# The output and router stage and the expert stage of a decoder layer as one program

## Chip, cores and metric

One Trainium2 chip, one of its cores. The metric is the device time of one execution, in microseconds.

## What is computed

One step of a one-layer decoder for 512 prompt tokens and 8 x 8 sample tokens, 576 in all, with 1,024 features, in float32. Two token mixers work side by side, their outputs are concatenated and projected, and a mixture of experts follows. What matters here, cut from the reference:

```python
y = jnp.concatenate([gla_o, nsa_o], axis=-1) @ w_out          # output projection
xp = xp + mod_p[:, 2] * yp
hp2 = modulate(xp, g_ffn[l], mod_p[:, 3], mod_p[:, 4])        # norm, scale, shift
logits = h @ w_router + b_router                              # 32 experts
top_logit, top_idx = lax.top_k(logits, 4)
top_w = softmax(top_logit)
# the token/expert pairs are sorted by expert into blocks of 128 rows; for each block:
gate = jnp.minimum(xb @ w_gate[e] + b_gate[e], 7)
up = jnp.clip(xb @ w_up[e] + b_up[e], -7, 7)
y = ((up + 1) * gate * sigmoid(1.702 * gate)) @ w_down[e] + b_down[e]
# rows are weighed and added up per token, then the residual and a last norm
```

Each expert has three matrices of 1,024 x 1,024. An expert with more than 128 rows needs a further, "overflow", block.

## The kernel before

`STAGES` (L3281) lists seven stages. Each issues its instructions inside a block of its own and ends with `stage_done` (L123 to 127), which clears its semaphores and makes all engines wait for each other. The change concerns the last two.

**`output_and_router` (L2212).** Tokens come in five tiles (`TILES`): four of 128 rows and a last one of the 64 sample rows. TensorE goes through the tiles: `project_out(t)` (L2387) makes the second half of the output columns (L2398; for the last tile both halves, in two column groups, L2401), then for the tile before it `turn_rows` (L2404, eight transposes), `route` (L2409, the logits, with the turned rows as stationary operand, L2416) and for the one before that `ranks` (L2420, how many earlier rows chose the same expert). VectorE adds the residual (L2657 to 2660), multiplies by the scale (L2665), chooses the tile before's experts (`choose`, L2587), finishes the norm (L2671), then does `shares`, `take_rank` and `place` (L2602 to 2636): the latter writes 0/1 matrices that say which expert and which row of a block each token goes to. ScalarE copies the turned rows (L2509) and makes the norm's root and the softmax's exponents. Products of the 0/1 matrices (`table`, L2457 to 2464) give the table of tokens by block; `begin_sums` (L2445) makes the sum over a token's experts of share times `b_down`, which starts each row of the result in DRAM. After the table VectorE counts the blocks (L2695 to 2710): from the number of rows per expert it works out which expert each overflow block belongs to and how many blocks are used. GpSimd gathers block 0's rows from DRAM (L2369), and SyncE asks for the first six quarters of the expert weights (L2342) once all projections are done and the last tile is normed.

**`experts` (L2750).** One step per block. The weights stream from DRAM in quarters of 1 MB, twelve per block, into six landing places. Each quarter is rounded by ScalarE (`high_part`, L3079), the remainder is taken by VectorE (`rest_part`, L3167), and TensorE makes three products from it: 12 instructions of 512 columns per quarter (L2965). The two halves of a split quarter stand in a ring of four, so rounding quarter n waits until quarter n-4 is used. Step k on TensorE is: biases, the four gate quarters, the turns of the activation of block k-1 (L2973), the four up quarters, the turns of the rows of block k+1, the four down quarters of block k-1. VectorE also reads the gate (L3180) and the up product (L3186), makes the activation (L3191, L3194) and the remainders of the turned rows (L3171). Before step 1 there is an opening in which block 0's gate and up products are made, and `overflow` (L3015) makes the table entries of the overflow blocks, from matrices that `place_overflow` (L2191) writes. The loop's length and the experts of the overflow blocks are read from SBUF (`used_blocks`, L2829). With this input 32 blocks are used.

## Time and profile before

| | us |
|---|---|
| median of three runs | 1798.55 |
| lowest, highest | 1796.72, 1801.39 |
| the profiled execution, own time | 1795.53 |
| its span, first to last instruction | 1793.5 |
| mean granted TensorE clock | 0.964 |

The page of the profile gives each engine's busy time; the chain of waits gives what ended last; the windows give busy time, granted clock (1.00 is 2.4 GHz, 0.50 is 1.2 GHz) and DMA for a stretch; the timeline gives the instructions in order, with like ones merged. All times are from the start of the span.

### The profile page before, as it was taken

What the parts mean: (1) busy time and instruction counts of PE and PEld (TensorE: products, weight loads), DVE (VectorE), ACT (ScalarE), POOL (GpSimd) and SP (SyncE); (2) the same over time, 40 slices, a digit from 0 to 9 for tenths busy, and PEclk for the clock granted to TensorE, in tenths of its full rate; (3) what the DMA queues carried; (4) which work ended last, traced back from release to release, by engine and by line L of the source; (5) the groups of instructions that cost most, each with busy time, mean ns of one, the idle gap of its engine ahead of it and who ended that gap; (6) DMA issues with size and microseconds to landing.
All of it is one profiled execution on the core that took longest, in us unless ns stands there. A gap on an engine that the chain in (4) does not pass through costs nothing.

```text
span 1793.5 us, 27031 instructions
## 1 busy us (share of the span) xinstructions
PE 1688.0 (94%) x9028; PEld 1312.8 (73%) x9028; DVE 1425.5 (79%) x1361; ACT 1099.8 (61%) x1045; POOL 333.4 (19%) x309
## 2 busy tenths in 40 slices
PE   4999978888998799999999999999999999999996
PEld 2776767555554478888888888888888888888884
DVE  4422564476426789999999999999999999999997
ACT  4212343455333367777777777777777777777773
POOL 0000021300101012223222222322222232223211
PEclk9999989699999689999999999999999999999998
DMA  9454553620226579999999999999999999999993
GB/s 348 172 185 171 107 156 101 209 96 7 77 87 200 219 269 355 382 371 377 375 378 376 371 377 376 373 375 375 378 371 381 377 373 376 382 374 374 386 351 125
DMA packets 114598, 516.08 MB, mean 288 GB/s; under 512 B 25870, under 2 KB 47710, under 8 KB 62058
## 3 DMA queue, kind: packets, MB, share of 16 engines
q1 hardware_dynamic: 101082, 483.48, 71.5%
q0 software_dynamic: 12800, 29.45, 5.9%
q10 hardware_dynamic: 656, 2.36, 0.3%
q8 instruction: 36, 0.59, 0.1%
q14 instruction: 24, 0.20, 0.0%
HBM read 502.75 MB, written 31.09 MB: 298 GB/s over the span
## 4 chain that ended last, share of the span: by engine, by line
PE 62%; DVE 1%; DMA 1%; ACT 0%; issue 0%; SPq 0%; POOL 0%; DVEq 0%; POOLq 0%; ACTq 0%
PE banks L2965 58%; PE banks L2973 3%; PE banks L2951 1%; DMA routing<-in_g_final 0%; DMA ffn_rows<-weighed,block_rows 0%; DVE split L3167 0%; DVE arena L3264 0%; PE banks L3020 0%; ACT split L3079 0%; DVE arena L3257 0%; DVE arena L3256 0%; SPq L2885 0%; POOL wait_taken L2903 0%; DVEq L2831 0%; DVE gates L3180 0%
## 5 line engine op out<-in xcount | busy, mean ns | idle before, releaser
L2965 PE MATMUL banks<-split 128*128 128x512 f32 x4608 | 1076.0, 393 | 1.1 <-DVE split L3167 1.1
L2965 PEld LDWEIGHTS banks<-split 128*128 128x128 f32 x4608 | 860.4, 188 | 185.9 <-issue 7.2
L3167 DVE TENSOR_TENSOR split<-expert_buffers,split 128x2048 fp32r<-128x2048 f32 x384 | 864.8, 2284 | 41.7 <-ACT split L3079 39.5
L3079 ACT ACTIVATE split<-expert_buffers 128x2048 fp32r<-128x2048 f32 x384 | 733.2, 1918 | 216.6 <-PE banks L2965 212.2
L2903 POOL TENSOR_TENSOR wait_taken<-routing 128x1 f32<-128x1 f32 x62 | 76.4, 1232 | 811.8 <-PE banks L2973 464.5
L2926 POOL DMA_INDIRECT ffn_rows<-weighed,block_rows x31 | 107.7, 3473 | 4.8 <-issue 4.8
L662 PE MATMUL banks<-w_in_high,hT_high 128*128 128x476 f32 x192 | 75.8, 395 | 4.6 <-DVE hT_low L498 4.6
L3171 DVE TENSOR_TENSOR split<-banks,split 128x1024 fp32r<-128x1024 f32 x64 | 77.8, 1215 | 0.7 <-ACT split L3082 0.7
L662 PE MATMUL banks<-w_in_high,hT_low 128*128 128x476 f32 x192 | 73.3, 382 | 0.0
L3082 ACT ACTIVATE split<-banks 128x1024 fp32r<-128x1024 f32 x64 | 64.5, 1008 | 6.1 <-PE banks L2973 6.1
L573 DVE COPY arena<-banks 128x476 f32<-128x476 f32 x12 | 7.8, 654 | 70.0 <-PE banks L662 69.9
L662 PE MATMUL banks<-w_in_low,hT_high 128*128 128x476 f32 x160 | 60.5, 378 | 0.0
L1873 ACT ACTIVATE arena<-banks 128x512 f32<-128x512 f32 (+1 forms) x45 | 24.5, 586 | 56.9 <-PE banks L2129 19.3
L1561 ACT ACTIVATE arena<-banks,arena 128x128 f32<-128x128 f32 (+3 forms) x64 | 33.2, 526 | 39.0 <-DVE arena L1587 38.8
L662 PEld LDWEIGHTS banks<-w_in_high,hT_high 128*128 128x128 f32 x192 | 36.7, 191 | 22.2 <-issue 17.0
L3110 ACT ACTIVATE weighed<-banks,block_weights 128x1024 f32<-128x1024 f32 x31 | 34.7, 1119 | 29.3 <-PE banks L2965 29.3
L3096 ACT ACTIVATE sigmoids<-gates 128x1024 f32<-128x1024 f32 x32 | 34.0, 1063 | 26.2 <-DVE gates L3180 26.2
L2908 POOL TENSOR_TENSOR routing<-routing 128x1 int32<-128x1 int32 x31 | 40.7, 1314 | 16.7 <-issue 9.1
L840 POOL MEMSET arena<- 128x2560 f32 x1 | 2.2, 2239 | 214.1 <-POOLq L127 214.1
L2973 PEld LDWEIGHTS banks<-routing 128*128 128x128 f32 x256 | 33.9, 192 | 10.0 <-DVE bias_ones L3162 7.5
L662 PEld LDWEIGHTS banks<-w_in_high,hT_low 128*128 128x128 f32 x192 | 36.6, 191 | 5.7
L2973 PE MATMUL banks<-routing 128*128 128x128 f32 x256 | 34.5, 279 | 6.7 <-DVE bias_ones L3162 6.7
(396 smaller groups left out, 1733.2 us busy)
## 6 DMA issues: line engine op xcount, KB each, us to landing
expert_buffers<-in_w_gate SPq DMA_DIRECT2D x128, 1024.0 KB, 7.8
expert_buffers<-in_w_up SPq DMA_DIRECT2D x128, 1024.0 KB, 17.9
expert_buffers<-in_w_down SPq DMA_DIRECT2D x128, 1024.0 KB, 7.4
arena<-in_w_ada SPq DMA_DIRECT2D x16, 1024.0 KB, 4.9
w_in_landing<-in_w_in SPq DMA_DIRECT2D x5, 1904.0 KB, 8.9
arena<-in_w_ada SPq DMA_DIRECT2D x4, 2048.0 KB, 19.8
arena<-in_x_prompt SPq DMA_DIRECT2D x8, 512.0 KB, 9.4
arena<-in_cache_cmp SPq DMA_DIRECT2D x32, 128.0 KB, 2.9
```

The source lines that it names most:

```text
L662: last = pe.matmul(ps[0:n, 4 + t, 0:CW], h[:, kt, t0:t0 + n].bitcast(F32R), w.bitcast(F32R), start=(kt == 0 and j == 0), stop=(kt == KT - ...
L2903: pool.tensor_tensor(sums[s_sum.index(sem)], one, one, ALU.add).then_inc(sem, 1)
L2908: pool.tensor_tensor(tokens, core.row_of[:, bass.ds(k, 1)], none, ALU.add).then_inc(s_tok, 1)
L2926: pool.indirect_dma_start(core.ffn_d, bass.IndirectOffsetOnAxis(ap=row_out.bitcast(U32), axis=0), y, None, bounds_check=NTOK - 1, oob_is_e ...
L2965: last = pe.matmul(ps[:, bank + c, :], x[:, kt * P:(kt + 1) * P].bitcast(F32R), wt.bitcast(F32R), start=(m == 2 and kt == 0 and x is xs[0] ...
L2973: last = pe.transpose(ps[:, TB + kt // 4, (kt % 4) * P:(kt % 4 + 1) * P], v[:, kt, :], ident)
L3079: act.activation(high[:, j % RING_Q].bitcast(F32R), v, ACT.Copy).then_inc(s_high, 1)
L3082: act.activation(dst.bitcast(F32R), ps[:, TB:TB + 2, :].rearrange("p b n -> p (b n)"), ACT.Copy).then_inc(sem, 1)
L3096: act.activation(s, g, ACT.Sigmoid, scale=ALPHA).then_inc(s_sig, 1)
L3110: act.activation(y, ps[:, DB:DB + 2, :].rearrange("p b n -> p (b n)"), ACT.Copy, scale=weight_out).then_inc(s_y, 1)
L3167: dve.tensor_tensor(rest[:, j % RING_Q].bitcast(F32R), v, high[:, j % RING_Q], ALU.subtract).then_inc(s_rest, 1)
L3171: dve.tensor_tensor(lo.bitcast(F32R), ps[:, TB:TB + 2, :].rearrange("p b n -> p (b n)"), hi, ALU.subtract).then_inc(out, 1)
```

## The change

The two stages become one stage, `output_and_experts`, without the barrier between them: `router_programs` returns one program per engine, and each engine's expert program starts by calling it. In detail:

- The logits are made with `w_router` as stationary operand, in four groups of 32 columns; ScalarE copies the result, and a product with a stacked identity adds the four groups and turns the result back.
- Between the products of tile 3 and the turn of the last tile stand 24 transposes of the identity whose result isn't used (`keep_busy(24)`).
- Ranks are taken and tiles placed one tile sooner; the choice for tile 3 moves behind the last norm; tiles 3 and 4 are placed together. The 0/1 products run in fp32r, with the weight as two parts in three planes.
- Block 0's rows are no longer gathered from DRAM: `first_rows(t)` multiplies each normed tile with a matrix that marks the rows of expert 0. Blocks 1 to 31 are known to be experts 1 to 31, so weights and loops up to there need no count.
- Tables, turned shares and the bias sums stand between the quarters of the opening, on TensorE, ScalarE and VectorE; the last bias sum stands in step 1.
- Counting the blocks and placing the overflow moves to step `COUNT_AT = 16` of the loop, ahead of that step's remainders on VectorE; TensorE's overflow product stands after that step's up product, and its down product waits for the overflow table. `used_blocks` is read after step 16.
- Rounding, remainders and turns of block 0 and 1 are done in halves (`first_rows_T`, `first_rest_T`). The first three quarters of weights are asked for when all projections are done, the next three after the last norm.

The diff, cut to its core (`...` marks what is left out):

```diff
+COUNT_AT = 16
-STAGES = [project, gla, compress, prompt_attention, sample_attention, output_and_router, experts]
+STAGES = [project, gla, compress, prompt_attention, sample_attention, output_and_experts]
...
+        def keep_busy(n):
+            pe.wait_ge(s_ht, ST)
+            for _ in range(n):
+                pe.transpose(ps[:, 0, 0:P], ident, ident)
         def route(t):
...
             for kt in range(KT):
-                last = pe.matmul(ps[0:n, 2, 0:NE], h2T[:, kt, 0:n], wr[:, kt, :],
-                                 start=(kt == 0), stop=(kt == KT - 1))
-            last.then_inc(s_lp, 1)
+                c = kt % 4 * NE
+                last = pe.matmul(ps[c:c + NE, 2, 0:n], wr[:, kt, :], h2T[:, kt, 0:n], start=(kt < 4), stop=(kt >= KT - 4))
+            last.then_inc(s_lgp, 1)
+        def add_groups(t):
...
+            pe.matmul(ps[0:n, 2, P:P + NE], lgT[:, 0:n], stacked, start=True, stop=True).then_inc(s_lp, 1)
+        def first_rows(t):
+            n = TILES[t][1]
+            pe.wait_ge(s_in_first, t + 1)
+            v = h2[t].rearrange("s (p k) -> s k p", k=KT)
+            for kt in range(KT):
+                last = pe.matmul(ps[:, 6 + kt // 4, (kt % 4) * P:(kt % 4 + 1) * P], v[0:n, kt, :], in_first[t][0:n, :],
+                                 start=(t == 0 and kt % 4 == 0), stop=(t == ST and kt % 4 == 3))
...
+        for t in range(NT):
+            project_out(t, range(KT // 2))
+            if t >= 2:
+                ranks(t - 2)
+            project_out(t, range(KT // 2, KT))
...
+            if t >= 1:
+                turn_rows(t - 1)
+                route(t - 1)
+                if t >= 2:
+                    first_rows(t - 2)
+                add_groups(t - 1)
+        keep_busy(24)
+        turn_rows(ST)
+        ranks(ST - 1)
+        route(ST)
+        add_groups(ST)
+        first_rows(ST - 1)
+        ranks(ST)
+        first_rows(ST)
+        ranks(NT)
...
+            def first_block():
+                pe.wait_ge(s_ones, 1)
+                pe.wait_ge(router.s_lg, NT)
+                pe.wait_ge(router.s_cnt, 1)
+                start_with_bias(0, 1, GB)
+                start_with_bias(1, 1, UB)
+                pe.wait_ge(s_xt, 1)
+                product(0, (xh, xl), GB, 0, range(2))
+                pe.wait_ge(s_xt, 2)
+                product(0, (xh, xl), GB, 0, range(2, 3))
+                tables()
+                product(0, (xh, xl), GB, 0, range(3, 4))
+                turn_shares(range(ST))
+                turn_shares(range(ST, NT))
+                product(1, (xh, xl), UB, 4, range(1))
+                begin_sums(0)
+                product(1, (xh, xl), UB, 4, range(1, 2))
+                begin_sums(1)
+                product(1, (xh, xl), UB, 4, range(2, 3))
+                begin_sums(2)
+                turn_rows(1, first=True)
+                product(1, (xh, xl), UB, 4, range(3, 4))
+                begin_sums(3)
...
 # TensorE, step(k, prev, last, counted)
                 up(k, first_of(prev) + 4)
+                if counted:
+                    pe.wait_ge(s_y, prev)
+                    overflow()
...
-            with pe.Fori(2, nb1) as k:
+            with pe.Fori(2, COUNT_AT) as k:
+                step(k, k - 1)
+            step(COUNT_AT, COUNT_AT - 1, counted=True)
+            pe.wait_ge(s_counted, 1)
+            nb, nb1, nb2, _ = used_blocks(pe)
+            with pe.Fori(COUNT_AT + 1, nb1) as k:
                 step(k, k - 1)
...
 # VectorE
             rest_part(0, None)
-            rest_T(xh, xl, s_xh, 1, s_xt)
-            for j in range(1, 6):
+            take_rank(ST)
+            take_counts()
+            first_rest_T(0)
+            dve.wait_ge(router.s_bo, 16)
+            rest_part(1, None)
+            last_shares()
+            rest_part(2, None)
+            last_places()
+            rest_part(3, None)
+            table()
+            for j in range(4, 6):
                 rest_part(j, None)
...
+            shares_low()
             read_gate(0, 4)
...
 # VectorE, step
+                if count:
+                    count_blocks(core, dve, linker(dve, s_dve, dve_count)).then_inc(s_counted, 1)
+                    place_overflow(core, dve, linker(dve, s_dve, dve_count)).then_inc(s_over, 1)
                 for j in range(4, 7):
                     rest_part(j, prev)
                 read_gate(k, at + 4)
-                if is_zero(prev):
-                    dve.wait_ge(s_ob, 1)
-                    write_table(core, dve, linker(dve, s_dve, dve_count), NE, NSLOT, DB).then_inc(s_tab, 1)
                 rest_part(7, prev)
                 rest_T(ah, al, s_ah, k, s_at)
                 for j in range(8, 11):
                     rest_part(j, prev)
                 read_up(k, at + 8)
+                if count:
+                    dve.wait_ge(s_ob, 1)
+                    write_table(core, dve, linker(dve, s_dve, dve_count), NE, NSLOT, DB, WIDE).then_inc(s_tab, 1)
                 activate(k)
...
 # ScalarE
             high_part(0, None)
-            rows_T(0)
-            for j in range(1, 6):
+            router_rows_T(ST)
+            weights(ST - 1)
+            high_part(1, None)
+            weights(ST)
+            first_rows_T(0)
+            for j in range(2, 7):
                 high_part(j, None)
...
+            shares_T()
             sigmoid(0)
             high_part(7, None)
+            begin_read(0)
+            high_part(0, 0)
+            begin_read(1)
+            high_part(1, 0)
...
```

`count_blocks` holds what L2695 to 2710 did. `place_overflow` as before, with a third plane of marks and one more slot.

## Rows read from the trace of the kernel before

**Rows 1.** The page: TensorE's busy time, share of the span and instructions.
```profile
PE 1688.0 (94%) x9028; PEld 1312.8 (73%) x9028; DVE 1425.5 (79%) x1361; ACT 1099.8 (61%) x1045; POOL 333.4 (19%) x309
```
**Rows 2.** Chain of waits, in the expert loop: start, us, engine, line.
```profile
1086.63 11.15 PE banks L2965 x48
...
1121.72 11.15 PE banks L2965 x48
```
**Rows 3.** Windows, one step of the loop: busy per engine, PEclk, DMA share, GB/s.
```profile
1110.17:1145.26 35.09, 35.09 (x166) 28.84 (x166) 33.78 (x19) 26.74 (x17) 9.01 (x7) 1.00 0.99 381
```
**Rows 4.** Timeline of one step: start, us, engine, line, operation, out<-in [idle before].
```profile
1083.01 11.08 DVE L3167 TENSOR_TENSOR split<-expert_buffers,split 128x2048 fp32r<-128x2048 f32 x5
...
1086.24 0.40 PE L2951 MATMUL banks<-block_biases,bias_ones 3*128 3x512 bf16 x4
...
1097.63 1.05 PE L2973 MATMUL banks<-routing,ups 128*128 128x128 f32 x8
...
1110.25 11.14 PE L2965 MATMUL banks<-split 128*128 128x512 f32 x48
...
1111.09 1.22 DVE L3186 TENSOR_SCALAR ups<-banks 128x1024 f32<-128x1024 f32 x1
```
**Rows 5.** Timeline of the seam between the two stages.
```profile
600.57 1.28 DVE L2671 SCALAR_TENSOR_TENSOR arena<-arena 64x1024 f32<-64x1024 f32 x1
...
627.33 1.91 ACT L3079 ACTIVATE split<-expert_buffers 128x2048 fp32r<-128x2048 f32 x1 [4.36 <-PEq L127]
...
629.55 2.06 POOL L2908 TENSOR_TENSOR routing<-routing 128x1 int32<-128x1 int32 x1 [9.13 <-issue]
...
633.30 20.90 PE L2965 MATMUL banks<-split 128*128 128x512 f32 x84
...
659.08 4.67 PE L3020 MATMUL banks<-arena 128*128 128x34 f32 x40
...
664.00 12.78 PE L2965 MATMUL banks<-split 128*128 128x512 f32 x48
...
689.22 11.14 PE L2965 MATMUL banks<-split 128*128 128x512 f32 x48
```
**Rows 6.** Timeline of the output stage: turns, projections, router product, last tile's residual.
```profile
573.37 7.11 PE L2398 MATMUL banks<-arena 128*128 128x512 f32 x16
...
580.32 1.05 PE L2377 MATMUL banks<-arena 128*128 128x128 f32 x8
...
582.55 1.97 PE L2416 MATMUL banks<-arena 128*128 128x32 f32 x16 [1.17 <-ACT arena L2509]
...
584.49 7.09 PE L2401 MATMUL banks<-arena 128*64 128x512 f32 x32
...
594.89 0.68 DVE L2653 TENSOR_TENSOR arena<-banks,arena 64x512 f32<-64x512 f32 x1
```
**Rows 7.** Timeline: first and last instruction of a choice, of the count, of the placing.
```profile
598.77 0.19 DVE L2590 TENSOR_TENSOR arena<-banks,arena 128x32 f32<-128x32 f32 x1
...
600.11 0.37 DVE L2599 TENSOR_REDUCE arena<-arena 128x32 bf16<-128x128 f32 x1
...
618.20 0.18 DVE L2697 TENSOR_SCALAR arena<-arena 128x32 f32<-128x32 f32 x1
...
622.14 0.18 DVE L2710 CAST routing<-arena 1x54 int32<-1x54 f32 x1
...
648.80 0.82 DVE L2194 TENSOR_TENSOR arena<-arena 128x640 f32<-128x640 f32 x1
...
652.53 0.51 DVE L2202 TENSOR_TENSOR arena<-arena 128x340 f32<-128x340 f32 x1
```
**Rows 8.** Windows of 5 us at the seam (columns as in rows 3).
```profile
595.00:600.00 5.00, 4.30 (x26) 4.11 (x25) 4.69 (x11) 2.51 (x4) 0.00 (x0) 0.57 0.01 2
...
630.00:635.00 5.00, 2.25 (x8) 1.52 (x9) 5.00 (x4) 5.00 (x4) 2.85 (x3) 0.50 0.46 151
635.00:640.00 5.00, 5.00 (x20) 4.01 (x20) 4.38 (x3) 2.98 (x2) 1.61 (x1) 0.83 0.82 317
```

More of the change, by code:

```diff
@@ new lines, in gpsimd @@
+    def gpsimd(pool):
+        link = linker(pool, s_pool)
+        pool.memset(core.none, 0).then_inc(s_first, 1)
+        pool.memset(core.xg, 0.0).then_inc(s_first, 1)
+        pool.wait_ge(s_b, 32)
+        for a in range(3):
+            if a < 2:
+                link(pool.tensor_copy(bparts[:, a, :], b32))
+                link(pool.tensor_tensor(b32, b32, bparts[:, a, :], ALU.subtract))
+            else:
+                pool.tensor_copy(bparts[:, a, :], b32).then_inc(s_bp, 1)
+        pool.wait_ge(s_bp, 1)
+        pool.dma_start(core.bias_d.rearrange("e q a m n -> (e q) (a m n)"), bparts.rearrange("p a n -> p (a n)")
+                       ).then_inc(s_bo, 16)
+        pool.wait_ge(s_first, 2)
+        pool.wait_ge(s_h2o, 16 * NT)
+        pool.wait_ge(s_tab, 1)
@@ L2747, with output_and_experts @@
 RING_Q = 4
-def experts(core):
+COUNT_AT = 16
+def output_and_experts(core):
+    router = router_programs(core)
     nc, io, ps = core.nc, core.io, core.psum
@@ L2836, in _ @@
         def _(sp):
+            router.sync(sp)
             def expert(k):
@@ L2874, in step @@
                 quarters(2, e, prev, 8)
+            step(1, 0)
+            with sp.Fori(2, COUNT_AT + 1) as k:
+                step(k, k - 1)
+            sp.wait_ge(s_counted, 1)
             nb, nb1 = used_blocks(sp, 2)
-            step(1, 0)
-            with sp.Fori(2, nb) as k:
-                step(k, k - 1)
+            with sp.Fori(COUNT_AT + 1, nb) as k:
+                step(k, k - 1, expert)
             e = expert(nb1)
@@ L2896, in _ @@
         def _(pool):
[L2897 removed]
+            router.gpsimd(pool)
             def take_waits(sem, n):
@@ L2932, in _, with step @@
             add_rows(1, 0)
-            pool.wait_ge(s_tab, 1)
-            with pool.Fori(4, nb) as k:
+            def step(k):
                 gather(k)
@@ L2974, in turn, with gate @@
                 last.then_inc(sem, 1)
-            def gate(k, before):
-                pe.wait_ge(s_xt, k + 1)
-                if not is_zero(k):
-                    pe.wait_ge(s_g, k)
-                    pe.wait_ge(s_u, k)
+            def gate(k, before, split=False):
+                pe.wait_ge(s_xt, 3 if split else k + 3)
+                pe.wait_ge(s_g, k)
+                pe.wait_ge(s_u, k)
                 start_with_bias(0, k + 1, GB)
                 start_with_bias(1, k + 1, UB)
-                product(0, (xh, xl), GB, before)
+                if split:
+                    product(0, (xh, xl), GB, before, range(2))
+                    pe.wait_ge(s_xt, 4)
+                product(0, (xh, xl), GB, before, range(2 if split else 0, 4))
             def up(k, before):
@@ L3035, in step @@
+            def step(k, prev, last=False, counted=False):
+                gate(k, first_of(prev), is_zero(prev))
+                if is_zero(prev):
+                    begin_sums(4)
                 turn_act(k)
                 up(k, first_of(prev) + 4)
+                if counted:
+                    pe.wait_ge(s_y, prev)
+                    overflow()
                 if not last:
                     turn_rows(k + 1)
-                down(k, prev, first_of(prev) + 8, last)
+                down(k, prev, first_of(prev) + 8, last, counted)
@@ L3107, in weigh @@
                 act.wait_ge(s_rowo, 2 * n)
-                if not is_zero(done):
+                if is_zero(done):
+                    act.wait_ge(s_begun[2], 32)
+                else:
                     act.wait_ge(s_yo, 16 * done)
@@ L3130, in step @@
                 sigmoid(k)
+                if is_zero(prev):
+                    begin_read(4)
+                    for i in range(2):
+                        act.wait_ge(s_begun[i], 32 - 16 * i)
                 acts_T(k)
@@ L3145, in _ @@
             step(1, 0)
-            with act.Fori(2, nb1) as k:
+            with act.Fori(2, COUNT_AT + 1) as k:
+                step(k, k - 1)
+            act.wait_ge(s_counted, 1)
+            nb, nb1, nb2, _ = used_blocks(act)
+            with act.Fori(COUNT_AT + 1, nb1) as k:
                 step(k, k - 1)
@@ L3162, in _ @@
             dve.memset(ones, 1.0).then_inc(s_ones, 1)
+            take_rank, last_shares, last_places, take_counts, shares_low, table = router.vector(dve)
             def rest_part(j, prev):
@@ L3236, in _ @@
             step(1, 0)
-            with dve.Fori(2, nb1) as k:
+            with dve.Fori(2, COUNT_AT) as k:
+                step(k, k - 1)
+            step(COUNT_AT, COUNT_AT - 1, count=True)
+            dve.wait_ge(s_counted, 1)
+            nb, nb1, nb2, _ = used_blocks(dve)
+            with dve.Fori(COUNT_AT + 1, nb1) as k:
                 step(k, k - 1)
```

968 lines of the change are left out of this document (502 added, 466 removed).

## The prediction

> **What bounds the kernel now.** I read the page first: TensorE has 94% of the span [rows 1]. The chain of waits then says where it ends last: from the expert loop onward it is nothing but TensorE, one step after another, each 35.09 us after the one before [rows 2]. The window of one such step shows TensorE busy for all 35.09 us at a granted clock of 1.00 and VectorE for 33.78 [rows 3]. Two things follow. What starts step 2 earlier by x makes the program x shorter, since nothing else ever catches TensorE up; and VectorE has only 1.3 us a step to spare, so work put on it inside the loop is paid as soon as its lead is used up. The lead is in the timeline of a step [rows 4]: the gate product starts at 1086.24, VectorE's run of five remainders ends at 1094.09, and the fifth of them (quarter 4, the first of the up product) is wanted when the turns of 1097.63 are over, at 1098.7. So the lead is 4.6 us.
>
> The timeline of the seam shows what a joint program can remove [rows 5]: the last tile is normed at 601.85, the expert program's first instruction starts at 627.33 and its first weight product at 633.30. Step 1's gate starts at 664.00 and step 2 begins at 700.36, when the down product of 689.22 ends. The bill is made against that 700.4.
>
> **Up to the last norm.** The output stage is bound by TensorE and VectorE together. A projection takes 7.1 us [rows 6]. Before the last one TensorE now also turns the first block's rows of tiles 0 and 1 by a product with a mark matrix: 16 instructions each, which cost 2.0 us by the 16 of the router product [rows 6], so 4.0 us. The router product itself falls from 1.97: with 64 columns per group, 32 instructions took 7.09 where 16 over the full width took 7.11 [rows 6], so two groups ran beside each other; for four I take 1.2 (bounds 0.5 and 2.0). That returns about 2 us over three tiles, and the extra product and ScalarE copy of each tile's logits take it back. The last projection ends some 4 us later than its 591.6, at 595.5. VectorE takes up that tile at 597.3 instead of 594.89 [rows 6], having placed tile 2 in between, but no longer chooses tile 3's experts ahead of the norm (1.7 us, 598.77 to 600.48 [rows 7]). The last norm ends at 603.0, 1.2 later than now; between 601.5 and 606.5 by the bounds.
>
> On column groups, the Trainium skill (TensorEngine Tiling (Array Packing), Performance Considerations) promises four-fold at 32 columns, but its Key Properties say that a change of tiling mode drains the engine. By the first the router product would take 0.5 us; by the second each product between full-width turns would pay twice for a drain, and no row here prices one.
>
> **From the last norm to the first weight product.** The 24 identity turns cost 3.1 us by the eight of 1.05 [rows 6] and, queued ahead of the last tile's turn, end at 604.7: 1.6 late. Then in a chain: turn 1.1, ranks of tile 3 0.3, copy 0.6, logits 0.8, copy 0.3, adding the groups 0.2, handovers 0.7, so 608.7; choosing 1.7; the first remainder, which VectorE's order puts there, 2.2; marking the last tile's first rows 0.5; turning them 2.2; counts 0.7; half of the split 0.7. The first weight product starts at 617, 16 us ahead of 633.3. The barrier, the overflow count, the table and the gather of block 0 are gone from this path; that is the gain meant.
>
> **How much of the 16 us reaches step 2.** VectorE gives much of it back. Between the last norm and the remainder before step 1's last gate quarter it has twelve remainders at 2.2 (26.8 [rows 4]) and, now in between, 22.0 of other work: two choices and two rank readings 5.6, both shares 2.7, placing two tiles at once 4.2, the table 0.8, the low shares 0.9, the four halves of two splits 2.8, reading gate and up 2.4, the activation 2.4, 0.2 for counts. That is 49 us, and I find 11 us of waits: for the last logits and turns 5.0, for the table 0.5, and 5.7 behind ScalarE, which now also sends out the expert bias sums between its roundings. Step 1's gate starts at 656.7 against 664.0. The last bias sum still sits in step 1 (0.5), and the first remainders of step 1 are late by what is left. Step 2 begins at 692.5: 7.8 earlier. That is with TensorE at full clock. The granted clock was 0.57 in 595 to 600, still 0.50 in 630 to 635, and 0.83 in 635 to 640, after the weight products had begun at 633.3 [rows 8]; TensorE's work between 600 and 620 is as sparse in the new order. If it runs at half clock until 622, the first product starts at 621.5 and the gain is 3.2. I take 6, the middle (bounds -2 and +12).
>
> **The count inside the loop.** At step 16 VectorE now does the block count and the overflow places before its remainder 4. The count took 618.20 to 622.32, 4.1 us, and the placing 648.80 to 653.04, 4.2 us [rows 7]. New in it are a third plane of 0.5, two small copies, the constants and one more slot: 1.2. So 9.5 us stand in front of remainder 4. Its lead of 4.6 doesn't cover this, but the price is not 9.5 less 4.6. The down product of step 16 also waits for the overflow table, and VectorE writes that only after it has read the up product. In a normal step the down product starts 24.0 us after the gate's bias, at 1110.25, while the up product is read until 1112.31 [rows 4], 26.1 after. All of VectorE's work up to there moves by 9.5 less its 0.9 of idle time, to 34.7; the table adds 0.8 and a handover. Down starts at 35.7 instead of 24.0: 11.7 us, in which TensorE's own overflow product (20 instructions, 2.3 by half of the 40 of 4.67 [rows 5]) is hidden. After that all engines fetch four block counts from SBUF; GpSimd's four took at most 2.2 us from the barrier's end to 629.55 [rows 5]. For TensorE I take 0.3, as its queue may be ahead (0 to 2.2). Together 12.0, between 10 and 14.
>
> **Sum.** -6 + 12 = +6 us on the profiled execution's 1795.53. The median of the runs is 3.0 above that execution, so 1798.55 + 6 = 1804.5. At nothing I cost: the first six quarters' loads, asked for at the last projection and the last norm as before; the write of the last 64 normed rows to DRAM, now behind 3 MB of them (wanted by rounding 2 at 616; cover about 3 us, and rounding 2 moves by what it lacks); the gather of block 1, whose cover is the wait for the up quarters, 8 us.
>
> **Rivals.** (A) *Same or faster:* the seam keeps its full gain. The first weight product is 16 us earlier; if ScalarE and VectorE interleave without the 11 us of waits, step 2 starts up to 16 earlier, and -16 + 11 gives 1793. It decides from 12 us of gain on. For it speaks that VectorE is idle 1.3 us a step only later; against, the 22 us of small operations placed between remainders. (B) *The count is cheaper:* if the table were ready before the down product, the stall would be the lead rule alone, 9.5 - 4.6 = 5, and the sum about -1: 1798. Against it stands the order of VectorE's program. (C) *The clock and a late norm:* half clock throughout the seam and TensorE as the bound of the output stage; no gain at step 2, or 2 lost, and 14 for the count: 1812 to 1815. (D) *The turns don't hold the clock*, so that part of the change does nothing: 24 turns at half clock as long as at full, gain 3, sum +9: 1807; it lies within the forecast.
>
> On the clock, the Trainium skill (TensorE: Matmul & The Clock Gate, Part 1) calls the throttled state the default that activity releases. By it the added turns would keep the 2.4 GHz level through the gap before the last turn, and the sum is that with 7.8 in place of 6, 1802.7; here the row of 595 to 600 has TensorE busy for 4.30 of 5 us at a granted clock of 0.57 [rows 8], so it is open whether the turns do it.
>
> **How the numbers follow.** Chances: forecast with D 0.58, A 0.14, B 0.13, C 0.15. What can be told from no change is 0.3%, 5.4 us. The forecast's own range is 1799 to 1810; A reaches down to 1793 and C up to 1815. 1795 to 1812 leaves out one in five. Faster by over 0.3%: half of A, with a little of B, 0.12. Slower: two thirds of the forecast and C, 0.54. Same: 0.34.
>
> **What would show it.** The first weight product near 617, step 1's gate near 657, step 2 near 692 to 697; every later step 35.09 long but for step 16, of some 47; in it a stall of TensorE before the up product and a longer one before the down product. Wrong if step 16 is under 42 us, if step 2 begins before 688, or if any other step is longer than 35.1.

## The result: slower by 0.2%, and the profile after

Over 20 executions of each on the same chips the changed kernel's median is 1802.51 us (1797.69 to 1808.00) and that of the kernel before 1797.74 (1793.17 to 1805.77). The ratio is 1.0021 with an interval of 1.0012 to 1.0031: slower by 2.2 to 5.6 us (3.8 by the ratio, 4.8 by the two medians), which so many runs can tell, though it is under the 0.3% that I had set as the limit. The profiled execution of after took 1802.55 us, its span is 1800.9 (before: 1793.5), at a mean granted clock of 0.968. These differ by 7.4, more than the medians, as the profiled execution of before lies 2.2 below its median of 20.

The page of after, as [rows 1]: TensorE still has 94%.

```profile
PE 1698.7 (94%) x9094; PEld 1319.9 (73%) x9094; DVE 1427.7 (79%) x1372; ACT 1101.0 (61%) x1052; POOL 337.3 (19%) x307
```

**The seam**, in TensorE's timeline of after, to be set beside [rows 5] and [rows 6] (start, us, engine, line, operation):

```profile
556.67 1.12 PE L2426 MATMUL banks<-arena 128*128 128x128 f32 x8
571.28 0.64 PE L2474 MATMUL banks<-arena 128*32 128x128 f32 x16 [1.17 <-ACT arena L2583]
571.86 4.09 PE L2506 MATMUL banks<-arena 128*128 128x128 f32 x16
600.16 4.17 PE L2506 MATMUL banks<-arena 128*128 128x128 f32 x16
604.42 3.29 PE L2464 MATMUL banks<-arena 128*128 128x128 f32 x24
607.64 1.10 PE L2426 MATMUL banks<-arena 64*128 64x64 f32 x8
615.49 4.20 PE L2506 MATMUL banks<-arena 64*128 64x128 f32 x16 [0.56 <-DVE arena L2689]
621.14 10.69 PE L3065 MATMUL banks<-split 128*128 128x512 f32 x36
657.37 0.61 PE L3051 MATMUL banks<-block_biases,bias_ones 3*128 3x512 bf16 x4 [3.94 <-DVE ups L3355]
657.91 13.75 PE L3065 MATMUL banks<-split 128*128 128x512 f32 x48
672.79 11.18 PE L3065 MATMUL banks<-split 128*128 128x512 f32 x48
695.68 0.40 PE L3051 MATMUL banks<-block_biases,bias_ones 3*128 3x512 bf16 x4
```

The first weight product starts at 621.1, 12.2 us ahead of the 633.3 of before; step 1's biases go out at 657.4, 6.3 ahead; step 2's at 695.7, 4.6 ahead of the 700.3 of before. So the seam gives 4.6 us, and the rest of the 12 is lost in the first two blocks. In block 0 it is 5.9 us: TensorE now has the tables, turned shares and bias sums between its quarters, and at 657.37 it waits 3.9 us for VectorE's reading of the up product. In step 1 it is 1.7: that step takes 38.3 us where it took 36.6 before. The 48 instructions behind the wait take 13.75, against 11.2 in a later step; but their like took 12.78 in the kernel before too [rows 5], behind no wait, so that only 1.0 of these 2.5 us counts against before. The bias sum moved into the step is 0.5 more.

From step 2 to the end each step takes 35.09 as in [rows 2], but for step 16, the one with the count. TensorE's timeline of it:

```profile
1186.89 0.40 PE L3051 MATMUL banks<-block_biases,bias_ones 3*128 3x512 bf16 x4
1187.22 11.22 PE L3065 MATMUL banks<-split 128*128 128x512 f32 x48
1198.28 1.05 PE L3073 MATMUL banks<-routing,ups 128*128 128x128 f32 x8
1203.95 13.83 PE L3065 MATMUL banks<-split 128*128 128x512 f32 x48 [4.61 <-DVE split L3336]
1217.61 2.42 PE L3124 MATMUL banks<-overflow_marks,slot_rows 128*128 128x54 f32 x20
1219.96 1.16 PE L3073 MATMUL banks<-routing 128*128 128x128 f32 x8
1221.94 11.14 PE L3065 MATMUL banks<-split 128*128 128x512 f32 x48 [0.82 <-DVE routing L2198]
1233.02 0.40 PE L3051 MATMUL banks<-block_biases,bias_ones 3*128 3x512 bf16 x4
```

Windows of step 16 and of the step ahead of it (columns as in [rows 3]; the PEclk is third from the end):

```profile
1151.80:1186.89 35.09, 35.09 (x165) 28.84 (x165) 33.78 (x19) 26.73 (x16) 9.17 (x7) 1.00 0.98 372
1186.89:1233.02 46.13, 40.70 (x186) 33.29 (x186) 44.34 (x53) 26.80 (x16) 10.66 (x7) 0.93 0.83 300
```

Step 16 took 46.13, so 11.04 over the others. Read off: 4.6 of waiting for remainder 4 (the first of the up product's quarters), 2.7 because the up product behind that wait took 13.83 for 11.17 (the granted clock was 0.50 from 1204 to 1208, and 0.93 over the step where it was 1.00), 2.4 for the overflow product, 0.8 for its table, and 0.5 of handovers. The bill of the two traces is thus -4.6 + 11.0 = +6.4; of the span's 7.4 about 1 is left, 0.8 of it behind the last instruction of VectorE, where only the stores of the result are left.

### The profile page after: what moved, and what is told of

The parts are those of the page before. It is cut to its first block, busy times and chain, and to the rows that moved or that the text cites. A ratio compares the mean times of both kernels' runs of the same rounds, so it can differ in the third digit from the quotient of the medians.

```text
span 1800.9 us, 26834 instructions
## 1 busy us (share of the span) xinstructions
PE 1698.7 (94%) x9094; PEld 1319.9 (73%) x9094; DVE 1427.7 (79%) x1372; ACT 1101.0 (61%) x1052; POOL 337.3 (19%) x307
## 4 chain that ended last, share of the span: by engine, by line
PE 62%; DVE 4%; DMA 1%; issue 1%; ACT 1%; SPq 0%; POOL 0%; ACTq 0%; POOLq 0%; DVEq 0%
PE banks L3065 55%; PE banks L3073 3%; DVE split L3336 2%; PE banks L2506 1%; PE banks L2448 1%; PE banks L3051 1%; DMA arena<-modulation 0%; DMA routing<-in_g_final 0%; DMA ffn_rows<-weighed,block_rows 0%; PE banks L2451 0%; ACT split L3221 0%; DVE arena L3456 0%; PE banks L2426 0%; ACT arena L2583 0%; DVE arena L3449 0%
## 5 line engine op out<-in xcount | busy, mean ns | idle before, releaser
L667 PEld LDWEIGHTS banks<-w_in_high,hT_high 128*128 128x128 f32 x192 | 36.6, 191 | 21.7 <-issue 16.6
L667 PEld LDWEIGHTS banks<-w_in_high,hT_low 128*128 128x128 f32 x192 | 36.6, 191 | 5.7
L3363 DVE TENSOR_TENSOR ups<-ups,sigmoids 128x1024 f32<-128x1024 f32 x32 | 39.3, 1229 | 1.1
L3360 DVE SCALAR_TENSOR_TENSOR ups<-ups,gates 128x1024 f32<-128x1024 f32 x32 | 39.2, 1226 | 1.1
```

Of the source, the lines that this page charges most:

```text
L667: last = pe.matmul(ps[0:n, 4 + t, 0:CW], h[:, kt, t0:t0 + n].bitcast(F32R), w.bitcast(F32R), start=(kt == 0 and j == 0), stop=(kt == KT - ...
L3360: dve.scalar_tensor_tensor(u, u, 1.0, g, ALU.add, ALU.mult).then_inc(s_t, 1)
L3363: dve.tensor_tensor(u, u, s, ALU.mult).then_inc(s_a, 1)
```

## Experiments

All edits are made to the kernel after, unless said. One thing has to be known to read them: the profiled executions differ by up to 6 us in when the output stage gets going, though nothing ahead of it was edited. The first tile's turn starts at 556.67 in the profiled execution of after, and between 556.46 and 562.67 in those below. Most of this has arisen in the stages before: VectorE's first instruction of the joint stage starts at 540.09 in after and between 537.88 and 544.47 below. The rest is a wait of VectorE's norm for the DMA of the modulation rows, which is absent in after and 0.3 to 2.1 us long in the others, as here in experiment 1:

```profile
554.83 1.23 DVE L2652 SCALAR_TENSOR_TENSOR arena<-arena 128x1024 f32<-128x1024 f32 x1 [1.31 <-DMA arena<-modulation]
```

So in a profiled execution I compare stretches that start at that turn or later (63.9 us from it to block 0's biases in after), not absolute times. One product of the first tile's second projection varies too with the clock of its moment: it takes 5.38 us in after and in experiment 4, 3.68 in experiments 1 and 6. Block 0's biases start at 620.60 in after, and it is 36.77 from there to step 1's and 38.31 on to step 2's.

The medians of 10 have intervals of some 2.5 us to either side, and those of experiments 1 to 4 all overlap with after's (ratio 1.0012 to 1.0031). So none of these four edits is told from after by its times alone; what each is worth is read from its trace.

**1. Without the identity turns.**

```diff
                 add_groups(t - 1)
-        keep_busy(24)
         turn_rows(ST)
```

> The 24 identity turns taken out, nothing else. In the changed kernel they ran from 604.4 to 607.7, while the last norm had ended at 603.7, so the last tile's turn stood behind them. My theory: they cost more than they hold. The first weight product (621.1 in the changed kernel) comes 2 to 3 us earlier, since the work up to it is loading of stationary operands, which does not depend on the granted clock; step 2's biases (695.7) come 1 to 3 us earlier and the time falls by as much. Rival: the turns are what held the clock at 0.96 in 605 to 610; without them it stays at 0.50 longer, the first product comes no earlier and step 2 not before 696.

Median of 10: 1799.20, ratio to before 1.0008 (0.9994 to 1.0022). From the first tile's turn to block 0's biases it took 59.6 in place of 63.9. Of these 4.3 us 1.7 are that varying product, so the turns cost 2.6. Block 0's biases at 618.58, step 2's at 693.48. Windows of 5 us of after, then of this run:

```profile
600.00:605.00 5.00, 5.00 (x32) 4.84 (x22) 3.56 (x6) 3.63 (x5) 0.00 (x0) 0.70 1.01 423
605.00:610.00 5.00, 4.37 (x51) 3.87 (x49) 2.16 (x11) 0.67 (x2) 0.00 (x0) 0.96 1.01 421
610.00:615.00 5.00, 4.63 (x23) 4.42 (x23) 3.74 (x10) 3.90 (x7) 0.00 (x0) 0.72 0.95 379
615.00:620.00 5.00, 4.51 (x21) 4.19 (x21) 0.88 (x4) 0.88 (x2) 0.00 (x0) 0.50 0.66 226
620.00:625.00 5.00, 4.45 (x14) 3.22 (x14) 4.71 (x10) 3.92 (x3) 0.00 (x0) 0.50 0.15 21
```

```profile
600.00:605.00 5.00, 4.77 (x35) 4.54 (x35) 3.86 (x4) 3.81 (x6) 0.00 (x0) 1.00 1.00 419
605.00:610.00 5.00, 3.78 (x37) 3.33 (x37) 3.65 (x20) 2.79 (x6) 0.00 (x0) 0.64 1.02 423
610.00:615.00 5.00, 4.45 (x23) 4.24 (x22) 3.43 (x6) 1.79 (x3) 0.00 (x0) 0.50 0.99 400
615.00:620.00 5.00, 4.45 (x23) 3.57 (x22) 1.87 (x4) 2.89 (x3) 0.00 (x0) 0.50 0.62 253
```

With the turns the clock is at 0.96 from 605 to 610 and without them at 0.64; by 615 it is at 0.50 in both. The last tile's turn starts at 607.64 in after and at 604.95 here, so the windows do not cover quite the same work. From that turn to block 0's biases it is 13.0 us in after and 13.6 here: the turns themselves take 3.3 and give back 0.7. Half of this 0.7 is a wait for tile 3's choice (0.8 us here), which they cover; the other half is the last tile's router product and the adding of its groups, 0.66 and 0.39 us here for 0.43 and 0.27. The long products of that stretch hardly depend on the clock (4.20 us at 0.50, 4.09 at full, the L2506 of the first fence). So the turns do hold the clock for a while, and cost 2.6 us net. The reason in my expectation holds for these long products only: the short ones do depend on it.

**2. The count spread over steps 4, 8 and 12**, its table and the overflow product still in 16.

```diff
 COUNT_AT = 16
+COUNTS = (4, 8, 12)
...
-                if count:
+                if k == COUNTS[0] if isinstance(k, int) else False:
                     count_blocks(core, dve, linker(dve, s_dve, dve_count)).then_inc(s_counted, 1)
-                    place_overflow(core, dve, linker(dve, s_dve, dve_count)).then_inc(s_over, 1)
+                if k == COUNTS[1] if isinstance(k, int) else False:
+                    place_overflow(core, dve, linker(dve, s_dve, dve_count), (0,))
+                if k == COUNTS[2] if isinstance(k, int) else False:
+                    place_overflow(core, dve, linker(dve, s_dve, dve_count), (1,)).then_inc(s_over, 1)
```

> VectorE's work for the overflow is spread: the block count in step 4, the first part of the placing in step 8, the second in step 12, each ahead of that step's remainders; the overflow product and its table stay in step 16. Step 16 took 46.13 us in the changed kernel against 35.09. My theory: each piece (4.1, 2.2 and 2.9 us) is within VectorE's lead of 4.6 us and costs nothing in its step; step 16 keeps the wait of the down product for the table behind the reading of the up product: 26.1 + 0.9 against 24.0, so 38 us. All together 8 us less than the changed kernel. Rival: the price is VectorE's work as such, wherever it stands, since it has only 1.3 us a step to spare: steps 4, 8 and 12 then take 38 to 39 us each and little is won.

Median of 10: 1800.40, ratio 1.0013 (0.9999 to 1.0028). Step 16 fell to 38.02 as expected, but step 4 took 37.00, step 12 35.69 and step 8 35.15: 5.5 us in all for what had cost 11.0, where I had expected 3. The rival's 38 to 39 for each of those steps did not come either. Between the ratios of after and of this run only 1.4 us are seen of the 5.5 that the traces show. The place where step 4 lost its 1.9 us, in TensorE's timeline:

```profile
791.07 8.42 PE L3069 MATMUL banks<-split 128*128 128x512 f32 x36
801.10 3.02 PE L3069 MATMUL banks<-split 128*128 128x512 f32 x12 [1.61 <-DVE split L3340]
```

It is not at remainder 4, whose lead of 4.6 covers the count's 4.1, but at remainder 11, the last quarter of the down product, which VectorE makes only after reading the up product and the activation. Of the 4.1 us, 0.9 is taken up by VectorE's idle time and 1.6 shows as a stall, so the lead there is about 1.6. The trace of the kernel before has the same, in the step of [rows 4]: this remainder ends at 1117.03, and the down product that starts at 1110.25 comes to its last quarter 8.4 us later, at 1118.7.

```profile
1114.75 2.28 DVE L3167 TENSOR_TENSOR split<-expert_buffers,split 128x2048 fp32r<-128x2048 f32 x1
```

That remainder, not the one I had looked at, sets what a step can take in.

**3. Overflow product and table early** in step 16: the product ahead of the up product, the table right behind the three remainders.

```diff
                 turn_act(k)
-                up(k, first_of(prev) + 4)
                 if counted:
                     pe.wait_ge(s_y, prev)
                     overflow()
+                up(k, first_of(prev) + 4)
```

```diff
                     rest_part(j, prev)
+                if count:
+                    dve.wait_ge(s_ob, 1)
+                    write_table(core, dve, linker(dve, s_dve, dve_count), NE, NSLOT, DB, WIDE).then_inc(s_tab, 1)
                 read_gate(k, at + 4)
...
                 read_up(k, at + 8)
-                if count:
-                    dve.wait_ge(s_ob, 1)
-                    write_table(core, dve, linker(dve, s_dve, dve_count), NE, NSLOT, DB, WIDE).then_inc(s_tab, 1)
```

> All of the counting stays in step 16, but TensorE's overflow product stands ahead of that step's up product, and VectorE writes the overflow table after three remainders, ahead of reading the gate. The wait of the down product for the table is gone. By my forecast's account (the table behind the reading of the up product is what makes 11 us of 5) step 16 falls from 46.1 to about 40. By the account that the trace of the changed kernel suggests, 11.0 is 4.6 for remainder 4, 2.6 for a lower granted clock after that stop, 2.4 for the overflow product, 0.8 for the table and 0.6 of handovers; then the overflow product now hides in the stop, and step 16 falls by 3 to 43.

Median of 10: 1799.86, ratio 1.0012 (0.9996 to 1.0027). Step 16 took 43.37, from 1190.70 to 1234.07:

```profile
1205.63 3.69 PE L3124 MATMUL banks<-overflow_marks,slot_rows 128*128 128x54 f32 x20 [2.49 <-DVE overflow_marks L2238]
1209.25 13.11 PE L3065 MATMUL banks<-split 128*128 128x512 f32 x48
1222.19 1.05 PE L3073 MATMUL banks<-routing 128*128 128x128 f32 x8
1223.00 11.14 PE L3065 MATMUL banks<-split 128*128 128x512 f32 x48
```

That is the 43 of the trace's account, not the 40 of my forecast's. TensorE waits 2.5 us for the overflow marks, and then the overflow product lies for 2.1 of its 3.6 us in the time that TensorE would have waited for remainder 4; the wait ahead of the down product is gone. It was 0.8 us for the table and 2.4 for the product that stood in the queue, and not the long table wait with the product hidden in it.

**4. The up product read ahead of the next block's first low rows**, before step 1.

```diff
             rest_part(1, 0)
-            first_rest_T(1)
             read_up(0, 8)
+            first_rest_T(1)
             activate(0)
```

> In the opening VectorE reads block 0's up product before it takes the remainders of block 1's turned rows, instead of after. In the changed kernel TensorE stood still from 653.4 to 657.4 before step 1's biases, which wait for that reading, and the granted clock was 0.66 in the 10 us after it. My theory: the biases start 1.5 to 2 us earlier; if the clock holds at 1.00 too, step 2 starts up to 4 us earlier, if not, 2. Rival: the split of the turned rows ends as late as before and sets the start of the gate product, so nothing changes.

Median of 10: 1800.63, ratio 1.0006 (0.9989 to 1.0023). From block 0's biases to step 1's 34.81 in place of 36.77, and on to step 2's 37.13 in place of 38.31: 3.1 us less in all. TensorE's wait there is 2.0 in place of 3.9, for the split of the turned rows now, and the first 48 instructions behind it take 12.79 in place of 13.75:

```profile
657.24 0.40 PE L3051 MATMUL banks<-block_biases,bias_ones 3*128 3x512 bf16 x4 [2.02 <-DVE split L3370]
657.56 12.79 PE L3065 MATMUL banks<-split 128*128 128x512 f32 x48
```

**5. Router logits over the full width again**, everything else as in after.

```diff
-                c = kt % 4 * NE
-                last = pe.matmul(ps[c:c + NE, 2, 0:n], wr[:, kt, :], h2T[:, kt, 0:n], start=(kt < 4), stop=(kt >= KT - 4))
-            last.then_inc(s_lgp, 1)
+                last = pe.matmul(ps[0:n, 2, P:P + NE], h2T[:, kt, 0:n], wr[:, kt, :], start=(kt == 0), stop=(kt == KT - 1))
+            last.then_inc(s_lp, 1)
```

> The column groups undone: the logits are made with the turned rows as stationary operand over the full width, as in the kernel before; ScalarE's copy of the logits and the product that adds the groups are gone. In the changed kernel the group product took 0.65 us for 16 instructions where the full-width one had taken 1.97. My theory: for the last tile the groups' way from the product's start to the choice takes 1.24 us (0.43, copy 0.22, sum 0.27, handovers), the full width 1.9 to 2.0, and TensorE has 1.0 us more for each earlier tile; the first weight product comes 1 to 3 us later and the time rises by as much, at most 3. Rival: the copy and the sum take back what the groups save, and nothing changes (within 0.5 us from the last norm to the first product).

Median of 4: 1811.16, ratio 1.0071 (1.0052 to 1.0089), which is 0.5% above after's, some 9 us (5 to 13 by the two intervals); both expectations had at most 3. From the first tile's turn to block 0's biases it took 70.3 for 63.9. The router product of the first four tiles in TensorE's timeline:

```profile
564.98 3.31 PE L2473 MATMUL banks<-arena 128*128 128x32 f32 x16 [1.18 <-ACT arena L2580]
579.40 1.97 PE L2473 MATMUL banks<-arena 128*128 128x32 f32 x16 [1.17 <-ACT arena L2580]
594.73 2.43 PE L2473 MATMUL banks<-arena 128*128 128x32 f32 x16 [1.17 <-ACT arena L2580]
611.56 2.21 PE L2473 MATMUL banks<-arena 128*128 128x32 f32 x16 [1.11 <-ACT arena L2580]
```

Against 0.65 each in after. From turn to turn a tile takes 14.5, 15.3 and 16.8 us here and 12.4, 13.9 and 14.3 in after, which makes 6.0 of the 6.4 us. Not all of the 6.0 is the form of the product: at full clock (579.40) it is 1.3 us longer than in after, about 4 us over three tiles, and the rest goes with a lower granted clock (0.56 under the product of 3.31, 0.80 under that of 2.43; half of the last projection took 4.55 at 0.79 for 3.65). Whether the edit brought the lower clock about isn't shown. So in the joint program it is TensorE that bounds the output stage, and what the router product is longer is paid, tile by tile; the copy and the adding of the groups, which I had set against it, lie on ScalarE and VectorE beside it and return nothing. The one new instruction pair of TensorE, L2481, takes 0.3 to 0.5.

**6. First rows turned from adjacent features.** The product that turns the first block's rows reads each row's features with a stride of 8 numbers; here it reads them adjacent, so that block 0 gets its features in a wrong order: the output is wrong, and the run shows times only. One execution.

```diff
-            v = h2[t].rearrange("s (p k) -> s k p", k=KT)
+            v = h2[t].rearrange("s (k p) -> s k p", k=KT)
```

> The products that turn the first block's rows read 128 adjacent features as stationary operand instead of every eighth one, so block 0 gets its features in a wrong order; everything else as in the changed kernel. There the 16 instructions of one tile took 4.09 us, at either granted clock, where I had counted 2.0 by the router product's 16 (stationary operand adjacent in SBUF). Theory: loading a stationary operand with a stride in a full float32 product costs twice; then a tile takes 2.0 to 2.2 us here, and the last norm and first weight product come up to 4 us earlier. Rival: it is the 128 moving columns (the router product had 32) that cost 4.09, and nothing changes.

It took 1797.92 us; from the first tile's turn to block 0's biases 55.3 for 63.9.

```profile
573.89 2.05 PE L2506 MATMUL banks<-arena 128*128 128x128 f32 x16
607.78 3.68 PE L2506 MATMUL banks<-arena 128*128 128x128 f32 x16
```

Those 16 instructions take 2.05 at full clock, as I had predicted for them, and 4.09 with the stride: the stride is the cause, and not the 128 moving columns, which are the same. At half clock (607.78) they take 3.68, where the strided ones take 4.20, nearly what they take at full clock. Of the 8.7 us less, 1.7 are the varying product of the first tile; 7.0 are left. From the first tile's turn to step 2's biases it is 130.8 for 139.0, so 6.5 us reach step 2 with that product taken off. The stride is thus the dearest single item of the seam, more than the turns and the late reading of the up product together (2.6 and 3.1), and experiments 7 and 8 still pay for it.

**7. All that helped, together**: no turns, the up product read first, table and overflow product early, and the count cut in six pieces of 1 to 2 us, one each in steps 3, 5, 7, 9, 11 and 13.

```diff
+PIECES = (3, 5, 7, 9, 11, 13)
...
+                piece = PIECES.index(k) if isinstance(k, int) and k in PIECES else None
+                if piece is not None:
+                    link = linker(dve, s_dve, dve_count)
+                    ins = (count_blocks if piece < 3 else place_overflow)(core, dve, link, piece % 3)
```

> Four edits on the changed kernel at once: no identity turns; up product read before the split of block 1's rows; VectorE's count and placing cut into six pieces of 1.2 to 2.2 us in steps 3, 5, 7, 9, 11 and 13; the overflow product ahead of step 16's up product, its table after three remainders. In the run with three pieces, the one of 4.1 us cost 1.9 in its step, a stop ahead of the last down quarter, where VectorE's lead is only 1.6 us; those of 2.2 and 2.9 cost 0.06 and 0.6. Theory: pieces of up to 2.2 us cost at most 0.2 each, step 16 takes 35.1 + 2.4 for the overflow product = 37.5; step 2 starts 5 us earlier than in the changed kernel, at about 690.5. In all 8.5 + 5 = 13 us less than the changed kernel, 7 to 9 less than the kernel before, ratio to it 0.9955. Rival: without the turns the clock falls in the opening and step 2 starts at 693, ratio 0.997.

Median of 5: 1790.95, ratio to before 0.9962 (0.9947 to 0.9977). Step 16:

```profile
1185.11 0.40 PE L3059 MATMUL banks<-block_biases,bias_ones 3*128 3x512 bf16 x4
1197.31 2.50 PE L3132 MATMUL banks<-overflow_marks,slot_rows 128*128 128x54 f32 x20
1222.62 0.40 PE L3059 MATMUL banks<-block_biases,bias_ones 3*128 3x512 bf16 x4
```

It takes 37.51, and steps 3 to 13 at most 35.15 each. All that is left of the count's 11 us is the overflow product's 2.5, and 0.1 in the steps of the pieces. The ratio lies between the theory's 0.9955 and the rival's 0.997, and its interval holds both. Step 2 starts at 693.8, but in this execution the first tile's turn starts 4.0 later than in after; from that turn to step 2 it is 133.1 us for 139.0, so 5.9 less. The rival's condition did not come: the granted clock was 1.00 from 655 to 670, and the 48 instructions behind the wait of 2 us took full speed:

```profile
657.62 0.40 PE L3059 MATMUL banks<-block_biases,bias_ones 3*128 3x512 bf16 x4 [2.05 <-DVE split L3378]
657.94 11.16 PE L3073 MATMUL banks<-split 128*128 128x512 f32 x48
```

**8. As 7, and ScalarE's order at the opening**: the last rounding of the first set and the first bias sum ahead of the sigmoid.

```diff
             shares_T()
-            sigmoid(0)
             high_part(7, None)
             begin_read(0)
+            sigmoid(0)
             high_part(0, 0)
```

> As the run with all four edits, and ScalarE rounds quarter 7 and sends out the first bias sum ahead of block 0's sigmoid. In the changed kernel VectorE waited 0.6 us for quarter 7 and TensorE 1.2 us for the first bias sum to be read. Theory: between the first weight product and step 1's biases 1 to 1.5 us less. Rival: the sigmoid, now later, delays the next rounding by as much, and nothing changes.

Median of 6: 1789.04 (1784.37 to 1791.69), ratio to before 0.9953 (0.9937 to 0.9969). From block 0's biases to step 1's 34.20 for the 35.55 of experiment 7, but step 1 takes 37.11 for 36.17, as the 48 instructions behind the same wait take 12.78 here for 11.16. So of the 1.35 us only 0.4 reach step 2 in these two executions, and the intervals of 7 and 8 overlap: that this order of ScalarE makes the program faster isn't shown. All of TensorE's waits from 618 to 1750:

```profile
PE banks L3059 <- DVE split L3378: 2.0, 1, 2.0
PE banks L2539 <- ACT arena L2632: 0.7, 1, 0.7
PE banks L3059 <- DVE arena L2782: 0.6, 1, 0.6
PE banks L3073 <- DVE split L3344: 0.4, 1, 0.4
```

Versions 7 and 8 both beat the kernel before, by 0.2 to 0.6% by their intervals, and the kernel after by more. The joint program is worth it, once what it moved is placed where there is room.

## Why the prediction was right or wrong

The sign and the two terms were right: a seam that gives less than it frees, and a count that costs more than that. The predicted 1804.5 is 2.0 above the measured 1802.51; I had forecast +6 and it is +3.8 (2.2 to 5.6). By my own limit of 0.3% that is "same", to which I had given 0.34, and not "slower", to which I had given 0.54. What was wrong lay inside, and much of it cancelled: that the number came so close is in part luck.

- **Last norm**, predicted to end at 603.0: 603.7. But by two wrong prices. The products that turn the first rows were put at 2.0 a tile, from the router product's row; they cost 4.1 (experiment 6: the stride). The router product was put at 1.2 and is 0.65, and the copies that I let take its gain back return nothing (experiment 5). The step that failed is the choice of the nearest row: same count, same type, but the stationary operand is read in another way. The two first-rows products ahead of the last projection thus cost 8.2 us where the forecast had 4.0, and the router products' gain, which it had cancelled, came in against it.
- **Turns**, predicted to hold the last tile's turn up by 1.6: it starts 4.0 us after the last norm's end, and without the identity turns 0.7 after it (experiment 1), so 3.3. They start at 604.4 and not at the forecast's 601.6, behind the first-rows product of 600.16. By the whole path they cost 2.6.
- **First weight product**, predicted 617 at full clock and 621.5 at half: 621.1. The clock was mixed, 0.96 in 605 to 610 and 0.50 in 615 to 620, so neither case was met. Of the 4.1 us after 617, 2.9 stand already at the last tile's turn (607.6 for 604.7), and that is the bullet above. From the turn to the product it is 13.5 for 12.3: the last tile's strided product took 4.20 where 2.2 had been counted, and VectorE waited 0.4 for the ranks behind the other one, while the rest was shorter than counted. That 621.1 stands beside 621.5 is luck.
- **Half clock as the reason** was therefore right only in part. By the Trainium skill (TensorE: Matmul & The Clock Gate, Part 1), I had written, the turns would keep the 2.4 GHz level through the gap and the sum would be 1802.7. The time comes out so, the mechanism doesn't: the windows of experiment 1 show the level held up to 610 and gone at 615, and the kernel without the turns is no slower. What came about is nearly rival D's result, that the turns do nothing for the seam, though not by its reason: they did hold the clock, while only short work ran.
- **VectorE's opening**, predicted as 49 us of work and 11 of waits up to the remainder for step 1's last gate quarter, 60 in all: its twelfth remainder ends at 664.03, 60.4 after the last norm, of which about 13 are waits, the longest of them 4.2 for the counts of the last tile. Step 1's gate started at 657.9 (predicted 656.7). What I had missed is that these are not one block of time: TensorE waited for a single reading of the up product that the program's order put behind less urgent work (experiment 4, 3.1 us).
- **Step 2**, predicted gain 6, called the middle of 7.8 and 3.2, which is 5.5: 4.6. Step 1 lost 3.2 against 35.09, of which I had named only the bias sum's 0.5. The other 2.6 go with the clock: the 48 instructions behind the wait of 3.9 us took 13.75 for 11.17, at 0.50 from 657.9 to 662. The kernel before had paid 1.6 of the same kind (12.78, [rows 5]), so against before step 1 lost 1.7. That row stood in my own list, and the sum didn't use it.
- **The count**, predicted 12.0 (10 to 14): 11.0. VectorE's piece was right, 9.2 us for 9.5. The down product started 35.05 after the gate's bias for 35.7. The step that failed is "TensorE's own overflow product is hidden" in one long wait for the table: the wait for remainder 4 was followed by a slower product (2.7), the overflow product (2.4) and only 0.8 of table wait. The sign that I had named, a longer stall ahead of the down product than ahead of the up product, is the wrong way round: 0.8 and 4.6. The sum is nearly the same since VectorE's order sets both ends, but the remedy is another, as experiment 3 shows with 43.4 where my account gave 40. The 0.3 for the block counts didn't show: step 17 begins right behind the down product.
- **The lead** of 4.6 was read correctly for remainder 4, but rival B took it for the step's; the smallest is 1.6, at remainder 11 (experiment 2). So B, at 5 us for the count, had the wrong rule even with another order of the program: experiment 3 meets its condition, a table ready ahead of the down product, and step 16 still cost 8.3.
- Rival A (the seam's full gain) and rival C (1812 to 1815) did not come about; though half clock, C's condition, held from 615 to 625.

**Open**: why the end of the program takes 1 us longer; where in the earlier stages the 6 us between executions arise; and what decides the granted clock. It was 0.70 in 600 to 605 of after while TensorE was busy for all 5 us of it, and behind one and the same wait of 2.05 us it was 1.00 in experiment 7 and 0.65 in 8.

## What to carry to other kernels

When work goes into a loop that one engine bounds and a second nearly fills, price it by the smallest lead of the second engine over the whole step, not by the one at the place of insertion, and cut it into pieces below that lead: here 11 us became 2.5, with the overflow product and its table moved as well. When two stages are joined, look at the first instruction that the bounding engine waits for and move it up in its producer's order; the 12 us freed at this seam were worth 4.6 until that was done, and 3.1 more with it. And take the price of a product from a row whose stationary operand is read in the same pattern.

## What the runs showed of the hardware that I had not expected

- A product of fp32 with a stationary operand of stride 8 takes twice as long: 4.09 us for 16 instructions of 128x128 against 2.05 with adjacent numbers (experiment 6). At half clock it is hardly longer (4.20), the adjacent one is (3.68).
- The 16 instructions of the router product in four column groups took 0.65 us for the 1.97 of the full width, three times as fast, and the full-width product behind them started 0.6 us after their first. The operands are swapped too (128 moving columns for 32), and no run separates the swap from the groups; but 16 full-width instructions with 128 moving columns took 2.05 (experiment 6), so the groups make the difference. The Trainium skill (TensorEngine Tiling (Array Packing), Performance Considerations) gives a factor of four at 32 columns; the drain that its Key Properties name is not visible in these rows.
- A stop of TensorE can cost again behind it, by a fall of the granted clock, but its length does not set the price. Behind waits of 3.9 to 4.6 us, 48 instructions took between 12.79 (experiment 5) and 13.84 (experiment 6), for 11.17 at full clock; behind waits of 2.0 us they took 12.79, 12.78 and 11.16 (experiments 4, 8 and 7); and in the kernel before they took 12.78 behind no wait [rows 5].
- The profiled executions differ by up to 6 us in when the first tile's turn of the output stage starts (556.46 to 562.67), more than the change itself does. At most 2.1 us of it are the wait for the DMA of the modulation rows; the stage itself starts up to 6.6 us apart.
